# Latent attention: the product with the values ahead of the turning of the probabilities, in odd slots

## The reference

```
kv = (rmsnorm(c_kv, kv_norm_g) @ w_ukv).reshape(b, s, MLA_HEADS, MLA_NOPE + MLA_V)
k_nope, v = kv[..., :MLA_NOPE], kv[..., MLA_NOPE:]
...
sc = (jnp.einsum('bqhd,bkhd->bhqk', qn, k_nope)
      + jnp.einsum('bqhr,bkr->bhqk', qr, k_rope))
p = jax.nn.softmax(sc.astype(jnp.float32) * scale, axis=-1).astype(v.dtype)
return jnp.einsum('bhqk,bkhd->bqhd', p, v)
```

## Time and profile before

| | us |
|---|---|
| median of 3 runs | 2822.15 |
| lowest, highest | 2821.24, 2824.7 |
| the profiled execution | 2823.3 |
| its span, first to last instruction | 2821.4 |
| the attention phase, first scores to last product with values | about 120 to 636 |

### The profile page before, as it was taken

One profiled execution on the slowest core, in us unless ns is written; L12 is line 12 of the kernel. 1 busy time (PEld: TensorE's weight loads), 2 busy tenths in 40 slices (PEclk: granted clock), 3 DMA queues, 4 the chain that ended last, 5 costly groups with the idle time before them and its releaser, 6 DMA issues. The chain is left out here.

```text
span 2821.4 us, 40156 instructions
## 1 busy us (share of the span) xinstructions
PE 2728.4 (97%) x13700; PEld 2270.0 (80%) x13700; DVE 1781.9 (63%) x2489; ACT 1349.6 (48%) x2089; POOL 1393.7 (49%) x1071
## 2 busy tenths in 40 slices
PE   8999999989999999999989999998898999999998
PEld 7788888877878888888867777786787888888886
DVE  6677777773665454555688888887428544555555
ACT  5577777763444444411356666665324444443112
POOL 1355555442587777644323222221236877775443
PEclk9999999999999999999999999999898999999998
DMA  3000000003122222522020000000321221225221
GB/s 139 26 10 8 7 7 10 15 1 141 68 90 74 82 89 84 206 90 106 29 114 31 31 31 31 30 23 23 157 97 45 89 89 67 89 84 214 89 89 60
DMA packets 54390, 195.33 MB, mean 69 GB/s; under 512 B 6544, under 2 KB 9872, under 8 KB 53776
## 3 DMA queue, kind: packets, MB, share of 16 engines
q1 hardware_dynamic: 54288, 193.95, 18.8%
HBM read 148.84 MB, written 45.09 MB: 69 GB/s over the span
## 5 line engine op out<-in xcount | busy, mean ns | idle before, releaser
L1315 PE MATMUL ffn_ps<-ffn_b,weights_hi 128*128 128x512 f32 x704 | 277.5, 394 | 16.2 <-issue 8.9
L1316 PE MATMUL ffn_ps<-ffn_b,weights_hi 128*128 128x512 f32 x704 | 276.3, 393 | 0.0
L1317 PE MATMUL ffn_ps<-ffn_b,weights_lo 128*128 128x512 f32 x704 | 276.0, 392 | 0.0
L1191 POOL TENSOR_TENSOR ffn_y_lo<-ffn_y_raw,ffn_y_hi 128x1024 fp32r<-128x1024 f32 x44 | 107.0, 2452 | 236.2 <-ACT ffn_y_hi L1112 236.2
L783 POOL TENSOR_TENSOR up_local_lo<-up_sums,up_local_hi 128x512 fp32r<-128x512 f32 x126 | 170.2, 1353 | 104.2 <-ACT up_local_hi L778 104.2
L409 POOL TENSOR_TENSOR weights_lo<-weights_raw,weights_hi 128x1024 fp32r<-128x1024 f32 (+2 forms) x64 | 124.3, 1948 | 189.0 <-ACT weights_hi L404 189.0
L2463 ACT ACTIVATE dif_p<-dif_s,dif_neg_max 128x1024 f32<-128x1024 f32 x128 | 142.2, 1113 | 136.1 <-DVE dif_neg_max L2671 117.5
L1315 PE MATMUL ffn_ps<-ffn_b,up_local_hi 128*128 128x512 f32 x504 | 196.1, 389 | 0.0
L1316 PE MATMUL ffn_ps<-ffn_b,up_local_hi 128*128 128x512 f32 x504 | 196.1, 389 | 0.0
L1317 PE MATMUL ffn_ps<-ffn_b,up_local_lo 128*128 128x512 f32 x504 | 196.1, 389 | 0.0
L1112 ACT ACTIVATE ffn_y_hi<-ffn_y_raw 128x1024 fp32r<-128x1024 f32 x44 | 44.1, 1050 | 315.0 <-PE ffn_ps L1317 315.0
(11 more groups left out here) (394 smaller groups left out, 8194.2 us busy)
## 6 DMA issues: line engine op xcount, KB each, us to landing
weights_raw<-in_up SPq DMA_DIRECT2D x44, 512.0 KB, 3.8
up_raw<-in_up SPq DMA_DIRECT2D x44, 512.0 KB, 4.2
ffn_products<-ffn_conv SPq DMA_DIRECT2D x44, 512.0 KB, 2.6
ffn_y_raw<-ffn_products SPq DMA_DIRECT2D x44, 512.0 KB, 4.0
ffn_down_raw<-in_down SPq DMA_DIRECT2D x24, 512.0 KB, 6.6
weights_raw<-in_diff_qkv SPq DMA_DIRECT2D x23, 512.0 KB, 3.5
weights_raw<-in_down SPq DMA_DIRECT2D x20, 512.0 KB, 6.1
x_spill<-x_in SPq DMA_DIRECT2D x16, 512.0 KB, 3.8
```

The costliest lines, as they stand in the source:

```text
L1315: pe.matmul(out, hi, x_hi, start=start, stop=False, skip_group_check=True)
L1316: pe.matmul(out, hi, x_lo, start=False, stop=False, skip_group_check=True)
L1317: return pe.matmul(out, lo, x_hi, start=False, stop=stop, skip_group_check=True)
```

## The change

In the slots of TensorE the block of V stands ahead of the block of T. Even slots have no V, and nothing changes there; odd slots run S, V, T in place of S, T, V. The waits move with their blocks. No instruction is added or taken away, on any engine.

```diff
                     mm.then_inc(scores_ready, 1)
-                if not (first and t < LAG_T) and (scores or t < LAG_T):
-                    m, tm = n - LAG_T, (t - LAG_T) % HT
-                    pe.wait_ge(probs_scaled, m + 1)
-                    if first and t == LAG_T:
-                        pe.wait_ge(values_act, QT)
-                        pe.wait_ge(values_dve, QT)
-                    for half in range(2):
-                        need(pe, pt_lo_done, 2 * m + (half - 1))
-                        for k in range(4):
-                            key = (4 * half + k) * P
-                            mm = pe.transpose(turn_ps[half][:, k * P:(k + 1) * P],
-                                              probs[tm % 4][:, key:key + P], cst[:, C_IDENT:C_IDENT + P])
-                        mm.then_inc(turned, 1)
                 if t % 2 == 1 and not (first and t < LAG_V):
                     p = 4 * h + (t - LAG_V) // 2
...
                     mm.then_inc(o_ready, 1)
+                if not (first and t < LAG_T) and (scores or t < LAG_T):
+                    m, tm = n - LAG_T, (t - LAG_T) % HT
+                    pe.wait_ge(probs_scaled, m + 1)
+                    if first and t == LAG_T:
+                        pe.wait_ge(values_act, QT)
+                        pe.wait_ge(values_dve, QT)
+                    for half in range(2):
+                        need(pe, pt_lo_done, 2 * m + (half - 1))
+                        for k in range(4):
+                            key = (4 * half + k) * P
+                            mm = pe.transpose(turn_ps[half][:, k * P:(k + 1) * P],
+                                              probs[tm % 4][:, key:key + P], cst[:, C_IDENT:C_IDENT + P])
+                        mm.then_inc(turned, 1)
```

## The result

The changed kernel is slower, by about 10 us. In six rounds beside the kernel before, it takes 2834.19 us (2832.14 to 2839.54) against 2824.47 (2821.24 to 2824.8): a ratio of **1.0039, 95% interval 1.0029 to 1.0049**. 2833.5 was forecast, against a before of 2822.15.

A forecast was written before the change was run, and what follows sets the result against it. TensorE, busy 97% of the span, was taken as the bound, with DVE and ACT in a chain. 12.3 + 1.3 + 0.9 - 1.4 - 1.3 = +11.8 us gave 2833.5 us, range 2821 to 2842.

The forecast's parts named there:

- The mechanism: Odd slots: T starts 1.92 us later, delaying ACT's copies, exponential, `take_o`, then DVE's sum and next row maximum.
- The row maximum of the even slot: DVE: cannot start before T + 3.88, T being the start of the odd slot's turning; 1.4 us late in slot 12.
- The four waits: TensorE: T of slots 4, 8, 14 and 0 waits 1.05, 0.65, 1.2 and 0.2 us more, 3.1 together.
- A steady pair of heads: Full pair in the attention phase: 3.1 us of new waits, 1.0 gone, +2.05; six such pairs +12.3.
- The first pair: No V before slot 5, so only slot 7's gain (0.6), slot 8 (0.65) and slot 14 (1.2): +1.3 us.
- The last pair and the tail: End of the attention phase: first half of the last pair +0.9 us, last head -1.4, tail -1.3.
- V giving way to T: TensorE boundary that the trace lacks: -0.08 to +0.08 us, 61 times, -5 to +5; taken as 0.
- T to V: TensorE: V's first product pays 0.08 us for coming behind transposes, 0.36 against 0.28 long.
- The reading of the earlier trace: Attention phase: DVE's waiting for ACT's `take_o` put at four times T's waiting for POOL's scaled probabilities.
- The plain gain: Rival, chance 0.09: even slots have more room than reckoned and only waits vanish, about -13 us, 2809.
- The draw: Rival, chance 0.12: only the waits of slots 4 and 14 arise, 0.6 us each; around 2822 us.
- The clock: Rival, chance 0.03: each 1.2 us wait costs about 4 us at 1.2 GHz, some 3 us, 14 times: +42, 2875.

The follow-up runs named there:

- combined: Against the kernel before: DVE's sum moved behind the next even slot's row maximum, V ahead of T only in slots 3, 7 and the last head: 2811.55 us, -13.1.
- sum_late: Against the changed kernel: DVE's sum of the V result moved to the next even slot, behind row maximum, shift and reciprocal: 2815.77 us, -9.0 against before.
- harm_slots: Against the kernel before: V ahead of T only in slots 1, 5, 11 and 13, other odd slots as before: 2846.25 us, +22.2.

## Why the prediction was right

- **The mechanism held.** ACT's copies behind T, the exponential behind them, `take_o`, DVE's sum, the next row maximum: each step is in the timeline of after at the place given. T + 0.64, 1.61, 2.84 and 3.37 against a predicted 0.64, 1.64, 2.90 and 3.43.
- **The row maximum of the even slot** starts at T + 3.72, not T + 3.88. I took 0.45 from the start of the sum to the next maximum; it is 0.35 where the maximum's scores are long there. This term was 0.1 too large, and it went into the waits of slots 8, 14 and 0 (slot 4's was reckoned by way of POOL's odd key).
- **The four waits** were predicted at 1.05, 0.65, 1.2 and 0.2 more than before; measured are 1.11 (slot 4), 0.65 (slot 8), 1.07 (slot 14, shown above) and 0.13 more (slot 0), 3.0 together. The waits of slots 1, 3 and 7 went, 1.1 us for a predicted 1.0. A steady pair of heads lost 1.85 us for a predicted 2.05, six pairs 11.5 for 12.3. The rows of slots 4 and 8, with the last product of S before each:

```profile
394.87 0.39 PE L420 MATMUL lat_s<-lat_key_hi,mat_q_lo 128*128 128x512 f32 x1
396.22 0.98 PE L2142 MATMUL mat_turn<-cst,mat_probs 128*128 128x128 f32 x7 [0.96 <-POOL mat_probs L1951]
...
410.96 0.39 PE L420 MATMUL lat_s<-lat_key_hi,mat_q_lo 128*128 128x512 f32 x1
411.85 0.87 PE L2142 MATMUL mat_turn<-cst,mat_probs 128*128 128x128 f32 x6 [0.50 <-POOL mat_probs L1951]
```

- **The first pair** was the term that was mis-sized: +0.4, not +1.3. Its slots 8 and 14 lose 0.3 and 0.8. The chain is shorter there: from T of slot 11 to T of slot 14 are 10.85 us against 11.11 in the fifth pair, and `take_o` to sum, for one, is 0.41 against 0.53. The last pair is like it (0.8 in slot 4 and 0.3 in slot 8). These two pairs are written out in the kernel, while the six are a loop, in which DVE's stream has register instructions between the others (75 in the length of one pair, and none in the first pair or the last). That these make the difference was not tested.
- **The last pair and the tail**: +0.9 - 1.4 - 1.3 = -1.8 predicted, -2.05 measured, and that it comes so near is luck. Slots 0 to 8 cost nothing in place of 0.9, slots 8 to 15 gave 1.75 for 1.4 (a period of two slots is 6.5 to 6.8 us for a predicted 6.85, and was 7.35, not 7.2), and from there to the last product the tail gave 0.3 for 1.3.
- **V giving way to T** was open between -0.08 and +0.08. It costs nothing: 0.12 from the last product of V to T, as between two products of V. This agrees with the Trainium skill (TensorE: Matmul & The Clock Gate, Architectural detail), by which TensorE can pull weight loads ahead of products in flight. Nor does T to V cost 0.08, as I had it; see the last section.
- **The reading of the earlier trace rows** was half of it. DVE's wait for `take_o`, 41.3 us, is not four times T's wait for POOL but about twice: 10.1 us stand in the row of TensorE's loads and 8.9 more in that of its products. Nothing in the sum rested on this.
- **The rivals.** The plain gain of 13 us is reached only by `combined`, where the sum no longer stands in the way and only useful slots are changed, and 6.0 of its 13 are had by moving the sum alone. The draw needed waits of 0.6 and they were 1.1. The clock did not fall in the steady pairs: granted 1.00 with two waits of 1.1 us in each (windows row of the changed kernel, columns as above). Its price was also too high: a stretch of 4 us at half the clock loses at most 2 us, not 3, which makes 28 and not 42 for 14 of them.

```profile
378.00:444.00 66.00, 63.44 (x405) 55.90 (x404) 49.09 (x95) 46.70 (x87) 33.13 (x42) 1.00 0.03 8
```

The sum came out at +11.8 for a measured +9.7, whose interval reaches from 8 to 14. In the phase itself it is 9.8, and 1.7 of the 2.0 too many are the six pairs (0.8) and the first (0.9).

## What to carry to other kernels

An instruction that is moved later on one engine is paid for in the streams of the engines that wait for it: read there what stands behind the waiting instruction, and behind who waits for that, until the path comes back to the first engine. Here a block of 2 us of cover took away 1.1 us of waits per pair of heads and made 3.0 of new ones, through a sum on DVE, which is busy for 49.1 of every 66 us there. Once the sum stood behind the row maximum, the same move cost nothing in the steady pairs of heads and saved some 2.5 us in the last pair and the tail; most of the 9.0 us of `sum_late` come from the sum's new place. And a delay is first met by the next consumer that has no cover; half of a change can therefore cost more than the whole (+22.2 us in `harm_slots` against +9.7).

## What was not expected of the hardware

- No boundary between products and transposes costs TensorE anything by starts. The 0.08 that the prediction has for the first product behind transposes (0.20 to the next one for 0.12, or 0.31 for 0.23) is made up for just before: that product starts 0.03 after the last transpose, where transposes are 0.11 apart. 0.03 + 0.20 is 0.11 + 0.12, and 0.03 + 0.31 is 0.11 + 0.23. The prediction took its lengths from start to start, so its sums stand. Transposes behind products, of either size, come when a further product would.
- In the tail of the changed kernel the clock fell some products after a wait of 2.01 us, the last of several (1.48, 0.21 and 0.65 before it): the products with the values come 0.12 us apart at first and 0.21 from the fifth of sixteen on. The granted clock is 1.00 from 636 to 642 and 0.50 from 643 to 646, the levels of 2.4 and 1.2 GHz. Waits of 1.1, 0.65, 1.1 and 0.3 us in each 66 had left it at 1.00. The last products of the changed kernel:

```profile
642.61 0.28 PE L2129 MATMUL mat_o<-mat_pt_lo,mat_v 128*128 128x256 f32 x1
642.73 0.29 PE L2127 MATMUL mat_o<-mat_pt_hi,mat_v 128*128 128x256 f32 x1
642.85 0.38 PE L2129 MATMUL mat_o<-mat_pt_lo,mat_v 128*128 128x256 f32 x1
643.03 0.42 PE L2127 MATMUL mat_o<-mat_pt_hi,mat_v 128*128 128x256 f32 x1
643.24 0.41 PE L2129 MATMUL mat_o<-mat_pt_lo,mat_v 128*128 128x256 f32 x1
...
645.38 0.41 PE L2129 MATMUL mat_o<-mat_pt_lo,mat_v 128*128 128x256 f32 x1
```
